# Prefill softmax: the normalization's multiplications by ScalarE instead of VectorE

## What is computed

```
def mla_expand(c_kv, w_kv_b, k_norm):
    kvb = (c_kv @ w_kv_b).reshape(b, S, MLA_HEADS, QK_NOPE + V_HEAD)
    k_nope = rmsnorm(kvb[..., :QK_NOPE], k_norm)
    return k_nope, kvb[..., QK_NOPE:]

def attend(q_nope, q_rope, k_nope, k_rope, v, q_pos, k_pos):
    s = (q_nope . k_nope + q_rope . k_rope) * ATTN_SCALE      # 16 heads
    s = jnp.where(mask, s, -inf)
    p = jax.nn.softmax(s, axis=-1)
    return p . v
```

## Time and profile before

| | |
|---|---|
| median of 3 runs | 1837.63 us (1836.75 to 1837.73) |
| profiled execution, its own time | 1838.07 us |
| its span, first to last instruction | 1836.3 us |
| mean granted TensorE clock | 0.999 of full speed |
| TensorE, VectorE, ScalarE, GpSimd busy | 99%, 62%, 45%, 12% of the span |

### The profile page before, as it was taken

The page is one execution under the profiler, slowest core; times in us unless marked ns, Lnnn a source line. Parts: engine busy times, 40 slices in busy tenths (PEclk is TensorE's granted clock), DMA queues, the critical chain, the costliest instruction groups (busy, mean ns, idle before and its releaser), DMA issues.

```text
span 1836.3 us, 28276 instructions
## 1 busy us (share of the span) xinstructions
PE 1809.4 (99%) x10567; PEld 1732.0 (94%) x10567; DVE 1135.3 (62%) x1706; ACT 827.9 (45%) x1420; POOL 228.4 (12%) x280
## 2 busy tenths in 40 slices
PE   9999999999999999999999999999998999999998
PEld 8999999799888999999999999996877999999998
DVE  6554447879889745444775554456778856454445
ACT  5333335665564433333563333346665544333333
POOL 1000010311312000011400001122112131000110
PEclk9999999999999999999999999999999999999999
DMA  6444444556452544444344444451124534444442
GB/s 212 132 120 134 141 138 151 155 207 231 125 206 87 188 131 123 128 145 137 119 138 124 129 123 138 138 173 40 47 80 142 170 116 128 132 121 130 144 137 76
DMA packets 68452, 249.48 MB, mean 136 GB/s; under 512 B 8264, under 2 KB 10568, under 8 KB 67088
## 3 DMA queue, kind: packets, MB, share of 16 engines
q1 hardware_dynamic: 58880, 206.86, 37.1%
q0 software_dynamic: 9488, 41.48, 6.7%
HBM read 235.51 MB, written 12.12 MB: 135 GB/s over the span
## 4 chain that ended last, share of the span: by engine, by line
PE 84%; DVE 8%; ACT 3%; issue 2%; DMA 2%; POOL 0%; SPq 0%; DVEq 0%; ACTq 0%; POOLq 0%
PE pair L1913 24%; PE pair L1914 24%; PE pair L1915 24%; DVE wlo L1245 2%; PE pair L2333 1%; PE pair L2335 1%; PE pair L2334 1%; PE pair L2425 1%; DVE cy L1372 1%; DVE S L1468 1%; DMA lowA<-in_cacheT 1%; PE pair L1920 0%; PE pair L1922 0%; PE pair L1921 0%; PE pair L2121 0%
## 5 line engine op out<-in xcount | busy, mean ns | idle before, releaser
L1913 PE MATMUL pair<-xh,whi 128*128 128x384 f32 x1960 | 660.4, 337 | 3.9 <-DVE xl L1255 2.9
L1915 PE MATMUL pair<-xh,wlo 128*128 128x384 f32 x1960 | 654.9, 334 | 0.0
L1914 PE MATMUL pair<-xl,whi 128*128 128x384 f32 x1960 | 654.9, 334 | 0.0
L1245 DVE TENSOR_TENSOR wlo<-raw,whi 128x1024 fp32r<-128x1024 f32 (+3 forms) x371 | 463.5, 1251 | 160.7 <-ACT whi L708 159.8
L708 ACT ACTIVATE whi<-raw 128x1024 fp32r<-128x1024 f32 (+2 forms) x369 | 378.2, 1028 | 262.0 <-PE pair L1915 258.0
L1913 PEld LDWEIGHTS pair<-xh,whi 128*128 128x128 f32 x1960 | 368.0, 188 | 11.2 <-issue 4.2
L1914 PEld LDWEIGHTS pair<-xl,whi 128*128 128x128 f32 x1960 | 368.0, 188 | 1.6 <-issue 1.0
L1915 PEld LDWEIGHTS pair<-xh,wlo 128*128 128x128 f32 x1960 | 368.0, 188 | 0.0
L1265 DVE TENSOR_TENSOR tg<-pair,rstd 128x384 f32<-128x384 f32 x88 | 49.0, 557 | 326.2 <-PE pair L1915 325.5
L1913 PE MATMUL pair<-ah,whi 128*128 128x384 f32 x704 | 235.2, 334 | 0.0
L1914 PE MATMUL pair<-al,whi 128*128 128x384 f32 x704 | 235.1, 334 | 0.0
(11 more groups left out here) (408 smaller groups left out, 2202.1 us busy)
## 6 DMA issues: line engine op xcount, KB each, us to landing
raw<-in_stream SPq DMA_DIRECT2D x372, 512.0 KB, 3.6
S<-in_ssm POOLq DMA_DIRECT2D x4, 2048.0 KB, 9.2
out_ssm_s<-S POOLq DMA_DIRECT2D x4, 2048.0 KB, 7.8
seg<-acs_rows POOLq DMA_DIRECT2D x12, 512.0 KB, 6.1
cTb<-in_cacheT POOLq DMA_DIRECT2D x10, 512.0 KB, 4.2
kn<-rs_rows SPq DMA_DIRECT2D x16, 264.0 KB
lowC<-in_cache SPq DMA_DIRECT2D x8, 512.0 KB, 3.2
lowA<-in_cacheT POOLq DMA_DIRECT2D x6, 512.0 KB, 5.5
```

Source lines behind the costliest of these rows:

```text
L1245: V.tensor_tensor(wlo[:, r, 0:w], raw[:, r, 0:w], whi[:, r, 0:w].bitcast(F32), ALU.subtract).then_inc(lo_ready, 1)
L1913: M(out, whi[:, r, ws], mh_(k), start=first and k == k0, stop=False)
L1914: M(out, whi[:, r, ws], ml_(k), start=False, stop=False)
L1915: ins = M(out, wlo[:, r, ws], mh_(k), start=False, stop=last and k == k1 - 1)
```

## The change

The two multiplications of `p_norm` leave VectorE, which keeps the reciprocal and signals it by the semaphore `dt_act`, renamed `dt_act_p_rcp` (its first two counts are used in the first layer as before, hence the offset of 2). ScalarE gets `p_scale(x)`: a wait for the reciprocal and two copies in place with the reciprocal as scale for each partition, the second of which signals `p_ready`. Heads 0 and 1 are scaled before the loop, behind `past_split(1)`; heads 2y+2 and 2y+3 behind squares 8y+6 and 8y+7 of group y, y = 0 to 6. In groups 1 and 2 that is behind L1144, in group 6 ahead of the Sqrt.

```
+            def p_scale(x):
+                s, o = x % 2, 48 + 8 * (x % 2)
+                act.wait_ge(dt_act_p_rcp, 2 + x + 1)
+                A(Pb[:, s, 0:128], Pb[:, s, 0:128], ACT.Copy, scale=sm[:, o + 6:o + 7])
+                A(Pb[:, s, 128:384], Pb[:, s, 128:384], ACT.Copy, scale=sm[:, o + 7:o + 8]).then_inc(p_ready, 1)
...
             past_split(1)
+            p_scale(0)
+            p_scale(1)
             for y in range(MH // 2):
                 for i in range(3):
                     past_square(8 * y + i)
...
+                if y + 1 < MH // 2:
+                    p_scale(2 * y + 2)
                 past_square(8 * y + 7)
+                if y + 1 < MH // 2:
+                    p_scale(2 * y + 3)
                 if y == MH // 2 - 2:
                     act.wait_ge(past_sum, 48)
...
             def p_norm(x):
                 s, o = x % 2, 48 + 8 * (x % 2)
                 dve.wait_ge(p_exp_ready, x + 1)
-                step(V.reciprocal(sm[:, o + 6:o + 8], sm[:, o + 4:o + 6]))
-                V.tensor_scalar(Pb[:, s, 0:128], Pb[:, s, 0:128], sm[:, o + 6:o + 7], None, ALU.mult)
-                V.tensor_scalar(Pb[:, s, 128:384], Pb[:, s, 128:384], sm[:, o + 7:o + 8], None, ALU.mult).then_inc(p_ready, 1)
+                V.reciprocal(sm[:, o + 6:o + 8], sm[:, o + 4:o + 6]).then_inc(dt_act_p_rcp, 1)
```

More of the change, by code:

```diff
@@ L281, in build @@
         dt_dve = sem("dt_dve")
-        dt_act = sem("dt_act")
+        dt_act_p_rcp = sem("dt_act_p_rcp")
         dtT_ps = sem("dtT_ps")
@@ L830, in dt_exps @@
                 step(A(dv[1], dv[0], ACT.Abs))
-                A(dv[2], dv[1], ACT.Exp, scale=-1.0).then_inc(dt_act, 1)
+                A(dv[2], dv[1], ACT.Exp, scale=-1.0).then_inc(dt_act_p_rcp, 1)
                 act.preload_act_table(ACT.Ln)
@@ L835, in dt_log @@
                 act.wait_ge(dt_dve, 3)
-                A(dv[6], dv[3], ACT.Ln).then_inc(dt_act, 1)
+                A(dv[6], dv[3], ACT.Ln).then_inc(dt_act_p_rcp, 1)
             def decay_rows():
@@ L1391, in dt_step @@
                 if i == 2:
-                    dve.wait_ge(dt_act, 1)
+                    dve.wait_ge(dt_act_p_rcp, 1)
                     V.tensor_scalar(dv[3], dv[2], 1.0, None, ALU.add).then_inc(dt_dve, 1)
@@ L1401, in dt_step @@
                     step(V.tensor_tensor(dtR[:, :, :], dtR[:, :, :], dv[5], ALU.add))
-                    dve.wait_ge(dt_act, 2)
+                    dve.wait_ge(dt_act_p_rcp, 2)
                     step(V.tensor_tensor(dtR[:, :, :], dtR[:, :, :], dv[6], ALU.add))
```

## The result

The changed kernel takes 1841.32 us (median of 11 runs, 1840.24 to 1843.89), the kernel before beside it 1837.73 us (11 runs, 1836.09 to 1839.34). The ratio is 1.0021, 95% interval 1.0013 to 1.0029: slower by 2.4 to 5.3 us. That is just about the 0.2% named as the bound, on both sides of it. The profiled execution has a span of 1840.2 us.

What follows compares the result with a forecast made beforehand. PE, busy 99% of the span, was taken to bound the kernel, with ScalarE's squares as the tight link. Terms 1.38 + 0.56 + 1.57 = 3.5 us took 1837.63 to 1841.1 us; range 1839.6 to 1843.0.

Steps and rivals of the forecast that it cites:

- the 0.2% named as the bound: Whole kernel: a measurement can tell about 0.2%, 3.7 us, from no change, so slower begins above 1841.3 us.
- The price of a pair: ScalarE: one p_scale, two scaled copies, holds it 0.69 us, from exps of the same shapes less overlap.
- The bounds without operand: ScalarE: lower price of a pair, 0.52 us, from Silu copies without a per-partition operand; would make the loss 2.6 us.
- (1) The start: Before the loop, ahead of the first square: two pairs go straight onto PE's path, 1.38 us lost.
- (2) Groups 0, 4 and 5: In these groups the pair of 0.69 us fits the 0.79 us gap before square 8y+7; cost 0.
- (3) Groups 1 and 2: Pairs behind the query-stack copy: group 1 loses 0.54 us, group 2's equal loss goes into group 3's existing waits.
- (4) Group 6: Ahead of the Sqrt table load: two pairs, 1.38, and 0.19 for the reciprocal wait delay square 56; 1.57 us lost.
- What is removed: VectorE: 32 multiplications, at most 11.1 us of busy time; PE waits for none of it, so worth 0.
- R1: After the loop: decode-attention waits give the slip back, kernel not slower, 1837.6 us; chance 0.08.
- R2: At new pauses near 1277.4 and 1376.8: PE's clock falls again, about 1.7 us more, 1842.8 us; chance 0.12.
- R3: ScalarE: pairs don't overlap with their neighbours, each takes 0.89 us, giving 1842.4 us; chance 0.12.
- R4: VectorE's relief reaches PE: waits on L1752 shorten by 0.55 us each, scalings hide, about 1836.7 us; chance 0.04.

Runs made afterwards that it cites:

- start_only: Only heads 0 and 1 scaled by ScalarE, ahead of the first square, the others on VectorE as in the kernel before; 1838.87 us against 1837.72, ratio 1.0007.
- roomy_only: Only heads 2, 3 and 10 to 13 scaled by ScalarE, the others on VectorE as in the kernel before; single run, 1836.68 us.
- group6_only: Only heads 14 and 15 scaled by ScalarE, ahead of the Sqrt table load, the others as in the kernel before; 1839.97 us against 1837.72, ratio 1.0011.
- group6_late: The changed kernel with heads 14 and 15 scaled behind squares 56 and 57, behind the Sqrt; 1840.23 us against 1838.47 for the kernel before, ratio 1.0012.
- no_scale: Multiplications of the prefill probabilities left out on both engines, VectorE only makes and signals reciprocals; 1838.35 us against 1838.47 for the kernel before, ratio 1.0001.
- group2_only: Only heads 6 and 7 scaled by ScalarE, behind group 2's query-stack copy, the others as in the kernel before; single run, 1837.08 us.
- all_in_gaps: The changed kernel with heads 0, 1, 4 to 9, 14 and 15 moved behind later squares; 1838.64 us against 1838.47 for the kernel before, ratio 1.0000.

## Why the prediction was right

The forecast was 1841.1 us and 3.5 us of loss; measured are 1841.32 us, 3.56 us in the loop, 3.9 us by the ratio. By its steps:

- **The price of a pair**, 0.69 us from the exps of the same shapes: 0.69 to 0.70 us at the start. The bounds without operand (0.52; the rows named there give 0.50, and the step from one to the other has no reason) and without overlap (0.89) were both wrong, the nearest rows right.
- **(1) The start**, 1.38 us: start_only +1.32 to +1.38, PE's wait 1.84 us against 1.85 forecast.
- **(2) Groups 0, 4 and 5**, nothing: roomy_only 0.00.
- **(3) Groups 1 and 2**, 0.54 us and 0 by absorption: 0.58 and -0.02. PE's new wait was forecast at about 0.65 us by the weight load and was 0.73; the loss in time, which is what counts, was right. The copy of the query stack does not overlap with the pair behind it either (1304.06 + 1.06, then 1305.14), as taken.
- **(4) Group 6**, 1.57 us: group6_only +1.49 to +1.55, and 1.60 between the changed kernel and group6_late.
- **What is removed**, nothing: no_scale -0.03.
- **That the slip reaches the end** (against R1): the loop lost 3.56 us, the medians differ by 3.59. That the two, and the forecast and the measured time, agree this closely is luck, since the interval reaches from 2.4 to 5.3 us. PE's wait in the decode attention that might have taken it, 2.3 us, reads 2.3 us in the changed kernel and in group6_late as well; it moves with the loop.
- **R2**, a further fall of PE's clock at the new pauses: not in the changed kernel's trace, where the granted clock is 1.00 behind both pauses (1.84 and 1.78 us by the weight load), nor in start_only, group6_only and group6_late, which have one of them each. **R3**, no overlap, falls with the pair's length, **R4** with no_scale.

The parts add up: 1.32 + 1.49 + 0.58 - 0.02 + 0.00 = 3.37 us one by one, 3.56 together. The missing 0.2 us are what single loops vary by: start_only, group6_only and group2_only each came out 0.06 to 0.07 us shorter in group 3, up to ScalarE's split of stream 4. The changed kernel's own trace adds up by itself. Measured from ScalarE's split of stream 1 to its splits of the streams behind it, it is 1.39 us behind the kernel before at stream 2 (the start), 1.95 at stream 3 (with group 1, 0.56 more), 1.97 at stream 4 (with group 2, 0.02), 1.99 at streams 5, 6 and 7 (with group 3, 0.02; groups 4 and 5, nothing), and 3.56 at the loop's end (with group 6, 1.57). Each term of the forecast stands there within 0.02 us. What the forecast could not settle is on which side of 0.2% the loss falls, and the measurement does not settle it either.

## What to carry to other kernels

An engine that is 45% busy can still have no room at one place: what counts is the gap in front of the instruction that the bounding engine waits for, here 0.79 us before a square in steady state, and nothing before the first square, behind another long copy, and ahead of a table load. Work put into the gaps was free within 0.03 us; the same work a few lines away in the queue cost its full length at the start and ahead of the table load, 0.6 us for a pair behind the long copy, and nothing where a later wait took the slip up. And before moving work off an engine, look whether anything waits for it there: leaving this work out altogether gained nothing.

## What the runs showed of the hardware

PE's clock. The pause of PE ahead of the second group of decode scores is, by the weight load, 2.3 us long in every trace (2.5 in one), and behind it the clock sometimes falls to 1.2 GHz (granted 0.50) and sometimes stays at 2.4 GHz. Windows of 2 us (busy us and instructions of PE, PEld, DVE, ACT, POOL; PEclk; DMA share; GB/s), first group6_only, where it stays:

```profile
1402.00:1404.00 2.00, 1.38 (x12) 1.14 (x11) 1.94 (x4) 0.00 (x0) 0.66 (x2) 1.00 0.12 42
```

then all_in_gaps, where it is down there and, in this one execution, a second time in the mixer, behind a wait of 2.1 us that stood in the kernel before too, without a fall:

```profile
342.00:344.00 2.00, 2.00 (x8) 1.96 (x7) 1.97 (x4) 1.97 (x3) 0.00 (x0) 0.50 0.33 35
...
1404.00:1406.00 2.00, 1.34 (x7) 0.97 (x6) 1.82 (x4) 0.00 (x0) 1.77 (x3) 0.50 0.48 78
```

Of the 12 profiled executions, 6 show the fall in the decode attention and 6 don't. From the loop's end to the first split of the decode output takes 88.5 to 90.9 us in the six with it (mean 89.6) and 87.8 to 89.9 in the six without (mean 88.4): 1.2 us between the means, beside a spread of 2 us within each half whose cause stays open. The fall does not go with the change: the kernels before and after both show it. The 12 traces are of 12 kernels, one each, but the mean granted clock differs between executions of one kernel too, as it would if the fall came and went there. Of the 19 executions of the kernel before that stand beside start_only, 7 have a clock of 1.000 and a median of 1836.64 us, 12 have 0.996 to 0.999 and 1838.45 us; in two further sets of 27 and 21 the same two medians lie 1.0 and 0.2 us apart. The 1.2 us are a third of what this change costs, and a reason to read such a change in the trace of its own stretch.
